# Modulation rows of a hybrid diffusion block: how 24 weight pairs are collected in PSUM and turned into columns

## The reference, cut to what matters

```python
sc, scc = jax.nn.silu(c), jax.nn.silu(c_ctx)
for layer in range(DEPTH):                       # DEPTH = 2, N_MOD = 6
    mod_l = jnp.split((sc @ ada_w[layer] + ada_b[layer])[:, None, :], N_MOD, axis=-1)
    mod_c = jnp.split((scc @ ada_w[layer] + ada_b[layer])[None, None, :], N_MOD, axis=-1)
    h_l = rmsnorm(x, norm1_g[layer]) * (1.0 + mod_l[1]) + mod_l[0]
    ...
```

## Time and profile before

| | |
|---|---|
| three runs, median | 2309.72 us |
| profiled execution, its own time | 2304.54 us |
| its span, first to last instruction | 2302.7 us |
| mean granted TensorE clock | 0.955 of full |
| PE busy | 2143.3 us, 93% of the span |
| DVE, ACT, POOL busy | 869.8, 451.3, 819.3 us |
| copies of rows (L1185) | 24, at 20.4 to 559.9 us |
| turnings (L593) | 24 of 8 records, at 21.9 to 572.2 us |
| `ada` (L579) | 24 of 16 records, at 14.8 to 550.6 us |

### The profile page before, as it was taken

One profiled execution on the slowest core, in us unless ns is written; L12 is line 12 of the kernel. 1 busy time (PEld: TensorE's weight loads), 2 busy tenths in 40 slices (PEclk: granted clock), 3 DMA queues, 4 the chain that ended last, 5 costly groups with the idle time before them and its releaser, 6 DMA issues.

```text
span 2302.7 us, 30202 instructions
## 1 busy us (share of the span) xinstructions
PE 2143.3 (93%) x11970; PEld 1710.9 (74%) x11970; DVE 869.8 (38%) x1249; ACT 451.3 (20%) x847; POOL 819.3 (36%) x439
## 2 busy tenths in 40 slices
PE   7989988999989978989999999997879998999997
PEld 3568657887877757878888888885656676888886
DVE  4543544212337774332121112233236664322334
ACT  3331111001344551031110001102005612100110
POOL 1443536121217765243222222224210034444442
PEclk8999998999989989989999999997889999999998
DMA  9434322333110011112111211122110012323222
GB/s 359 168 100 152 110 101 96 115 135 126 56 65 1 1 37 55 60 37 69 64 47 63 73 65 64 50 65 75 59 37 1 1 64 65 97 79 108 97 76 74
DMA packets 50840, 182.33 MB, mean 79 GB/s; under 512 B 5680, under 2 KB 5936, under 8 KB 49712
## 3 DMA queue, kind: packets, MB, share of 16 engines
q1 hardware_dynamic: 49296, 171.53, 22.1%
q10 hardware_dynamic: 928, 6.37, 0.8%
q0 software_dynamic: 512, 2.95, 0.4%
HBM read 178.72 MB, written 2.10 MB: 79 GB/s over the span
## 4 chain that ended last, share of the span: by engine, by line
PE 86%; DVE 6%; POOL 3%; ACT 2%; DMA 1%; issue 1%; ACTq 0%; DVEq 0%; SPq 0%; POOLq 0%
PE psum L512 21%; PE psum L517 21%; PE psum L513 21%; PE psum L1100 2%; PE psum L1088 2%; PE psum L1117 2%; PE psum L733 1%; PE psum L699 1%; PE psum L579 1%; PE psum L918 1%; POOL weights_lo L2129 1%; PE psum L943 1%; PE psum L535 1%; PE psum L662 1%; PE psum L541 1%
## 5 line engine op out<-in xcount | busy, mean ns | idle before, releaser
L2129 POOL TENSOR_TENSOR weights_lo<-weights,weights_hi 128x1024 fp32r<-128x1024 f32 (+1 forms) x232 | 515.4, 2222 | 1038.2 <-DVE weights_hi L1618 1038.2
L1618 DVE CAST weights_hi<-weights 128x1024 fp32r<-128x1024 f32 (+1 forms) x232 | 167.9, 725 | 919.8 <-PE psum L517 749.2
L517 PE MATMUL psum<-normed_lo,weights_hi 128*128 128x512 f32 x1760 | 508.6, 352 | 0.0
L512 PE MATMUL psum<-normed_hi,weights_hi 128*128 128x512 f32 x1088 | 394.0, 362 | 7.9 <-POOL weights_lo L2129 7.9
L513 PE MATMUL psum<-normed_hi,weights_lo 128*128 128x512 f32 x1088 | 375.3, 360 | 0.0
L517 PEld LDWEIGHTS psum<-normed_lo,weights_hi 128*128 128x128 f32 x1760 | 286.0, 190 | 16.7
L512 PEld LDWEIGHTS psum<-normed_hi,weights_hi 128*128 128x128 f32 x1088 | 205.8, 189 | 57.9 <-POOL weights_lo L2129 5.7
L512 PE MATMUL psum<-normed_first_hi,weights_hi 128*128 128x512 f32 (+1 forms) x672 | 234.1, 348 | 11.9 <-POOL weights_lo L2129 11.4
L513 PEld LDWEIGHTS psum<-normed_hi,weights_lo 128*128 128x128 f32 x1088 | 206.6, 190 | 36.1 <-issue 1.8
L513 PE MATMUL psum<-normed_first_hi,weights_lo 128*128 128x512 f32 (+1 forms) x672 | 214.6, 340 | 0.0
L512 PE MATMUL psum<-hidden_hi,weights_hi 128*128 128x512 f32 (+1 forms) x528 | 189.0, 358 | 0.0
(11 more groups left out here) (303 smaller groups left out, 3039.8 us busy)
## 6 DMA issues: line engine op xcount, KB each, us to landing
weights<-in_wall SPq DMA_DIRECT2D x264, 512.0 KB, 3.9
weights<-in_wall SPq DMA_DIRECT2D x32, 384.0 KB, 3.2
weights<-in_wall SPq DMA_DIRECT2D x32, 320.0 KB, 3.1
residual<-in_xT SPq DMA_DIRECT2D x1, 3072.0 KB, 14.3
residual<-in_xT ACTq DMA_DIRECT2D x1, 3072.0 KB, 9.8
phase<-in_tab ACTq DMA_DIRECT2D x2, 1280.0 KB, 5.5
out_T<-normed SPq DMA_DIRECT2D x2, 1024.0 KB, 4.3
normed<-in_window SPq DMA_DIRECT2D x1, 1536.0 KB, 8.7
```

The source lines that it names most:

```text
L512: mm(acc[:, lo:hi], WH[:, b, k, :], high[:, lo:hi], start=st, stop=False)
L517: ins = mm(acc[:, lo:hi], WH[:, b, k, :], low[:, lo:hi], start=False, stop=en)
L1618: dve.tensor_copy(WH[:, b, 0:n, :], W[:, s, HALF * b:HALF * b + n, :]).then_inc(w_hi, 1)
L2129: TT(WL[:, s, at, :], W[:, s, at, :], WH[:, b, 0:width(gs[0], b), :].bitcast(f32), ALU.subtract).then_inc(w_lo, 1)
```

## The change

Eight pairs now share one sum in bank 6. The stationary operand is a window of 32 columns in a wider `CS` (46 columns, the two vectors in columns 14 and 15), moved by two columns for each pair, so that pair `at` of a group writes rows 2 at and 2 at + 1 of each group of 32 rows and adds zeros to the others. One copy and one turning (4 matmuls that move 16 columns instead of 2) serve a group of eight pairs. There are three groups: pairs 0 to 7, 8 to 15 and 16 to 23. Their copies stand on ACT after the tiles of c = 1, before the first step of x0 and where the last copy stood; their turnings stand on PE after n = 6, in the first step of x0 and in the first step of xbc. The selector is made by POOL at the start, from three additions of parts of the identity, after the load of `consts`. `mods` reads `MODP` in a new order.

```diff
-        CS = region(25600, KT, 32)
+        CS = region(25600, KT, 46)
+        SEL = region(25968, 16)
...
-            def ada(gs, i):
+            def ada(g):
+                group, at = divmod(PAIR[g], 8)
+                if group and at == 0:
+                    pe.wait_ge(row_copied, group)
                 for part in range(2):
...
-                        if part == b == 0 and not (len(gs) == 1 and PAIR[gs[0]] == 0):
-                            pe.wait_ge(row_copied, along([PAIR[g] for g in gs], i))
                         for k in range(2):
-                            ins = mm(PS[rows, 6, :], CS[:, 4 * part + 2 * b + k, :],
+                            ins = mm(PS[rows, 6, :], CS[:, 4 * part + 2 * b + k, 14 - 2 * at:46 - 2 * at],
...
-                                     start=part == 0, stop=part == 1)
+                                     start=part == 0 and at == 0, stop=part == 1 and at == 7)
...
-            def flips(gs, i):
-                pe.wait_ge(row_copied, along([PAIR[g] + 1 for g in gs], i))
+            def flips(group):
+                pe.wait_ge(sel_ready, 1)
+                pe.wait_ge(row_copied, group + 1)
                 for q in range(4):
-                    ins = mm(dst, row[:, q * P:q * P + P], vec("sel", 0, 2), start=True, stop=True)
+                    at = 64 * group + 16 * q
+                    ins = mm(PS[:, 7, at:at + 16], ROWS[group > 0][:, q * P:q * P + P], SEL, start=True, stop=True)
...
             def fill():
-                if rows:
-                    flips([rows.pop()], 0)
-                if early:
-                    rows.append(early.pop(0))
-                    ada([rows[0]], 0)
+                ada(early.pop(0))
...
-                    if n in (3, 5, 6):
+                    if n in (3, 5):
                         fill()
+                    if n == 6:
+                        flips(0)
...
-                    flips([g - 2 for g in gs], i)        # uv; likewise in x0 and z
...
+                    if n == 0:                           # x0
+                        flips(1)
...
+            def copy_row(group, last):
+                act.wait_ge(blocks_done, 2 * last + 4)
+                if group:
+                    act.wait_ge(flipped, group)
+                run(ROWS[group > 0], PS[:, 6, :], ACT.Copy).then_inc(row_copied, 1)
...
-                    if n in (0, 3, 5):
-                        copy_row([AT["ada_a"] + 2 * (3 + (n + 1) // 3)], 0)
...
+            pool.wait_ge(c_in, 16)
+            TT(SEL, C[:, IDENT, 0:16], C[:, IDENT, 32:48], ALU.add).then_inc(g_ch, 1)
+            pool.wait_ge(g_ch, 1)
+            TT(SEL, SEL, C[:, IDENT, 64:80], ALU.add).then_inc(g_ch, 1)
+            pool.wait_ge(g_ch, 2)
+            TT(SEL, SEL, C[:, IDENT, 96:112], ALU.add).then_inc(sel_ready, 1)
```

More of the change, by code:

```diff
@@ L710, in _ @@
                         token_spread(6).then_inc(n_spread, 1)
-            assert not early and not rows
+            assert not early
             pe.wait_ge(kd_ev, 12)
@@ L737, in uv @@
             def uv(i, gs, between=None, by_tile=None, f=None):
-                def work():
-                    between()
-                    flips([g - 2 for g in gs], i)
-                two_blocks(gs, i, hn, between=between and work, by_tile=by_tile)
+                two_blocks(gs, i, hn, between=between, by_tile=by_tile)
                 if f is not None:
@@ L748, in uv @@
                     spectrum(0, f, 0, 4)
-                ada([g + 1 for g in gs], i)
+                ada(gs[0] + 1)
                 if f is not None:
@@ L811, in _ @@
                 g = AT["z"] + 3 * n
[L813 to L817, removed]
+                two_blocks([g], 0, hn, between=(lambda: inverse(6)) if n == 0 else None)
                 if n == 0:
                     inverse(7)
-                ada([g + 1], 0)
+                ada(g + 1)
             pe.wait_ge(g_ready, 8)
@@ L851, in _ @@
             for n in range(6):
-                two_blocks([AT["xbc"] + n], 0, hn, between=(lambda: flips([AT["xbc"] - 2], 0)) if n == 0 else
+                two_blocks([AT["xbc"] + n], 0, hn, between=(lambda: flips(2)) if n == 0 else
                            None if n == 5 else (lambda: transposes_x(2 * n - 2)))
@@ L1175, in _ @@
             act.wait_ge(eps_ready, 2)
-            run(CS[:, :, 0:2], V[:, _cols["cc"]:_cols["cc"] + 16].rearrange("p (k c) -> p k c", c=2),
+            run(CS[:, :, 14:16], V[:, _cols["cc"]:_cols["cc"] + 16].rearrange("p (k c) -> p k c", c=2),
                 ACT.Silu).then_inc(silu_c, 1)
[L1179 to L1185, removed]
+            def copy_row(group, last):
[3 more added lines that the diff above has]
+                run(ROWS[group > 0], PS[:, 6, :], ACT.Copy).then_inc(row_copied, 1)
             for layer in range(3):
@@ L1241, in _ @@
                     run(PS[:, 4 + n % 2, :], SD[:, 1, t, :], ACT.Square).then_inc(kg_sqd, 1)
[L1242 to L1243 removed]
+                if c:
+                    copy_row(0, AT["ada_a"] + 14)
                 for m in range(6):
@@ L1351, in x_by_token @@
                     run(XBC[:, k, :], XBC[:, k, :], ACT.Copy, scale=vec("dskip", k)).then_inc(dx_ready, 1)
-            copy_row([AT["xbc"] - 2], 0)
+            copy_row(2, AT["xbc"] - 2)
             act.wait_ge(dta_raw, 1)
@@ L1584, in mods @@
                 ab = V[:, _cols["ada_b"] + 48 * layer + lo:_cols["ada_b"] + 48 * layer + hi]
-                return TT(MOD[:, layer, lo:hi, :], MODP[:, layer, lo:hi, :],
-                          ab.unsqueeze(2).broadcast_to([P, hi - lo, 2]), ALU.add)
+                n = (hi - lo) // 4
+                rows = MODP[:, 0, :, 4 * layer:4 * layer + 4, :] if lo == 0 else MODP[:, 1 + layer, :, :, :]
+                return TT(MOD[:, layer, lo:hi, :].rearrange("p (a q) c -> p a q c", q=4),
+                          rows.rearrange("p q a c -> p a q c"),
+                          ab.rearrange("p (a q) -> p a q", q=4).unsqueeze(3).broadcast_to([P, n, 4, 2]), ALU.add)
             def gains(which, layer, m, name):
```

34 lines of the change are left out of this document (11 added, 23 removed).

## The result

Four runs of the changed kernel beside four of the kernel before gave 2290.01 us (2284.21 to 2295.2) against 2308.22 us (2306.3 to 2310.96): a ratio of 0.9922, with a 95% interval of 0.9898 to 0.9947, which is 12 to 24 us less. The direction was forecast.

The account below looks back on a forecast made before the run. PE was taken to bound the kernel, busy 93% of the span. Filter 2.37, squares 0.97, uv 5.53 and x0 to z 4.74 sum to 13.6 us, off 2309.7 gives 2296.1 us; range 2290.5 to 2302.

Parts of the forecast that it names:

- A turning costs PE 0.79 us at full clock: Each turning on PE takes 0.79 us, 8 records of 0.099 us, with 2 or 16 moving columns alike.
- The clock at the start: Removing two turnings before the filter's first products might change PE's granted clock; size taken as 0.
- Result of the sum: Whole kernel: 13.6 us taken off the 2309.7 us median gives 2296.1 us.
- The turnings on the path: Turnings that count in full: filter 2.37 us, uv 5.53 us, x0 to z 4.74 us.
- The squares: Filter, n = 3 and 5: squares of x no longer wait for `ada`; 0.97 us saved, bounds 0 to 2.5.
- rival A: Clock stays low into the filter's first products: 1.5 to 3 us lost, chance 0.10; all at half clock, 0.03.
- Hidden work: Start turnings, those in the first two x0 steps, POOL's selector, new waits and `mods` were put at 0.
- Rival B: uv does not pay, its steps 4 to 6 being tied to DVE and POOL: 5.53 us lost, 2301.6 us, chance 0.09.
- Rival D: Shifted window makes loading the stationary operand dearer, so the kernel is slower, 2314.4 us; chance 0.02.
- What was to show it: Fewer turning records, uv steps 19.6 us, z steps 18.9, filter's c = 1 1.8 us earlier, xbc 13.6 earlier.
- one of the signs of being wrong: Forecast wrong if modulation products exceed 1.85 us a pair, clock at 36 to 45 is 0.5, or POOL or a load takes over uv.

Follow-up runs that it names:

- before_look: The kernel before, unaltered, profiled once more for the clock: 10.65 us for the filter's first products, 27.40 us in step 7 of uv.
- t_start: Changed kernel with idle turnings put back before pairs 1 and 2 at the start: 2287.43 us, ratio 0.9917 to the kernel before.
- c_squares: Changed kernel with two ACT copies (of constants) and their waits for `ada` put back at n = 3 and 5 of the filter: 2291.12 us, ratio 0.993.
- second comparison: Six runs of the changed kernel with seventeen of the kernel before on one chip: 2290.48 against 2307.52 us, ratio 0.9932.
- again: The changed kernel, unaltered, timed and profiled once more: 2290.48 us, ratio 0.9932 to the kernel before.

## Why the prediction came out as it did

**The steps that failed.** "A turning costs PE 0.79 us at full clock" was too small: it measured 0.89 us at the 13 places in uv, x0 and z. The clock at the start was put at nothing ("I take 0"): it cost 1.9 us at least. And the base was too high: "Result of the sum" took the saving off 2309.7 us, the median of three runs, where the kernel before measures 2308.2 beside the changed one and 2307.5 over seventeen runs. The first two have opposite signs and nearly cancel, so the median came out under the range by the base (1.5 to 2.2 of the 6.1 us between point and result) and by a rest that stays open. The saving itself, 13.6 us, lies within the interval of both comparisons.

- **The turnings on the path.** The list of places was right: 3 in the filter, 7 in uv, 6 from x0 to z. In uv, x0 and z a turning is worth 0.89 us, since the matmul behind it pays 0.10 for it; 13 times that 0.10 is 1.3 us too little. I had 0.33 beside 0.23 in the chain of the kernel before, and read the 0.33 as L512's own. In the filter, where `ada` stands behind it, 0.78 was measured, as forecast.
- **The squares.** Forecast 0.97 us. At full clock the piece from pair 3's product to pair 4's shrank by 0.78 (before_look 20.46, t_start 19.68) and that from pair 4's to pair 6's by 1.26 (14.47 to 13.21). Of these 2.04 us, 0.78 is the turning after t = 1, counted apart, so this place gave 1.26 us. The way there was half right. The squares do come 2.7 us earlier against the products (6.92 and 4.23 us behind them), but c_squares gives only 0.50 us for the wait that the copies caused. The rest is the time of the turnings after n = 3 and n = 5 themselves, which were nearly on the path: PE idled only 0.17 us before 79.66. PE sets the pace up to pair 5's product and still waits 0.48 us for DVE before L655 (80.04).
- **Full-clock sum.** 13 x 0.89 + 3 x 0.78 + 1.26 = 15.2 us, where the forecast had 13.6 (the turning after t = 5 of c = 0 was not seen alone at full clock and is taken as the others).
- **The clock at the start, rival A.** It came true in its small form, in all nine profiles without work in that gap: 1.4 to 1.7 us for L655 partly at half clock, 1.9 us by where these products end. I took 0, and gave 1.5 to 3 us a chance of 0.10. The Trainium skill's rule (TensorE: Matmul & The Clock Gate, "What's actually happening": activity releases the throttle) was the right one to weigh, and I had the row for it: the gap in front of L662 was filled by exactly the work that the change takes away. That needed no luck to foresee.
- **Net.** 15.2 - 1.9 = 13.3 us: errors of opposite sign that bring the sum back to the forecast's 13.6. That the two agree is luck. The second comparison has 15.7 (12.5 to 18.7), the first 18 (12 to 24), so this sum lies inside both intervals. The profiled executions differ by 12.6 us (2304.6 on the mean of two, against 2295.2, 2287.86 and 2292.77), and they show where. On the mean pair 8's product starts at 143.5 us in the kernel before (145.13, 141.78) and at 143.7 in the changed one (144.13, 143.53, 143.38); pair 23's starts at 547.9 (548.70, 547.14) and at 536.3 (538.97, 534.98, 534.82). So the 11.7 us gained by then are the 13 turnings of uv to z (11.6), and in these profiles the clock took back all that the filter saved, 3.8 us and not only 1.9, if roughly, since the two profiles of the kernel before differ by 3.4 there. That makes 2 to 4 us of the 15.7 that no stage of the profiles explains. They stay open; the clock in uv and behind 572 us moves single executions by more than that.
- **Hidden work.** Pairs 0 and 1, the step before 388 us, POOL's selector, the new waits and `mods` cost or gave nothing that the traces show, the clock apart. Group 1's turning starts at 349.5 us while POOL works on until 354.9. Rival B did not come: steps 2 to 6 of uv, 4 to 6 included, are 0.87 to 0.90 us shorter. Rival D did not come: L580 has 1.85 us a pair as before, whatever the window. Its argument that a load of 128 columns takes under 0.2 us "whatever the tile" was too general (L619 of the kernel before has 277 ns), but nothing hung on it.
- **What was to show it.** 24 records of L591, three of the copy, 19.5 for 20.4 us in uv and 18.8 for 19.7 in z were there. The dated rows were not. PE's first products of c = 1, due 1.8 us earlier than 79.66, came at 80.04 (79.34 in again). The row at 388.51, due 8.9 us earlier, came at 385.34, 3.2 earlier. The last turning came at 561.97 for 571.64, 9.7 us earlier and not 13.6. This execution lost time to the clock at the start (about 2) and in the first interval of uv, from pair 8's product to pair 9's, which took 26.25 us against 23.57 before and 24.5 in two other profiles of the same kernel. And one of the signs of being wrong was there: the clock was to be 0.5 "at 36 to 45", and was so in the first part of it.

## What to carry to other kernels

A short group of matmuls on the path costs what the distance between two fixed marks shrinks by when it goes, not the length of its own piece in the chain; the instruction behind it can hold a part. Work in front of a stage that TensorE bounds can be worth having even where it hides: before taking it out, see what the granted clock will be when the stage starts, and keep some cheap matmuls in the gap if it falls. A kernel in which the clock falls in an idle time of TensorE in one execution and not in the next needs many runs and several profiles before 5 us mean anything.

## What the runs showed of the hardware

Matmuls without use, put into two idle times of about 2.5 and 3 us, made the first products of the next stage 1.5 to 1.6 us shorter (10.55 against 12.09 to 12.18); the time fell with them from 2290.48 to 2287.82 us, which alone is within the noise. In the nine profiles in which PE stood idle for 2.1 to 3.0 us in front of these products, the clock was at half in their first part; in the five in which it had work there (idle for 1.4 us at most) it was full. A matmul of 512 columns behind a turning takes 0.10 us longer than behind the six records of transposes of 128 columns (0.33 and 0.24 us). Of the same program, single executions place the half clock in different idle times: one step of uv took 24.8 us in one profile and 26.5 in another, with nothing in the program changed.
